# Part of one convolution job computed in float32 inside the first stage of a two-block transformer kernel

## The reference

```python
mod = silu(c) @ w_ada + b_ada                    # 2048 -> 6*2048, one row
h = rmsnorm(x, norm_mix) * (1 + sc_a) + sh_a     # 256 x 2048
p = h @ w_in                                     # 2048 -> 9296 columns
c_q, c_kv, k_pe, q_g, k_g, v_g, z, b_logit, a_logit, gate_logits = split(p)
y_a = mla(c_q, c_kv, k_pe, ...) @ w_o_mla        # latent attention, 8 heads
y_b = gdn(causal_conv_silu([q_g, k_g, v_g]), ...) @ w_o_gdn   # gated delta rule
```

## Time and profile before

| | |
|---|---|
| median of three runs | 2272.47 us |
| the profiled execution | 2270.37 us, of which the span shown in the profile is 2269.0 us |
| PE, PEld busy | 2191.9 us (97%), 1841.6 us (81%) |
| DVE, ACT, POOL busy | 1512.9 us (67%), 999.8 us (44%), 28.9 us (1%) |
| mean granted clock of TensorE | 0.989 of full |
| chain that ended last | PE 81%, DVE 9%, issue 3%, DMA 3%, ACT 3% |
| HBM | 503.56 MB read, 223 GB/s over the span |

### The profile page before, as it was taken

One profiled execution on the slowest core, in us unless ns is written; L12 is line 12 of the kernel. 1 busy time (PEld: TensorE's weight loads), 2 busy tenths in 40 slices (PEclk: granted clock), 3 DMA queues, 4 the chain that ended last, 5 costly groups with the idle time before them and its releaser, 6 DMA issues.

```text
span 2269.0 us, 27387 instructions
## 1 busy us (share of the span) xinstructions
PE 2191.9 (97%) x10608; PEld 1841.6 (81%) x10608; DVE 1512.9 (67%) x1898; ACT 999.8 (44%) x1263; POOL 28.9 (1%) x28
## 2 busy tenths in 40 slices
PE   6788999999998999999999999999999999999998
PEld 4678998788886788888888888887888888888886
DVE  7989888778867667765544555566556655655556
ACT  4355444433443464443344434456444444444444
POOL 0000000000000000000000000000000000000000
PEclk9899999999999999999999999999999999999999
DMA  9978747676899858986656556556666666566663
GB/s 361 403 260 241 253 151 268 216 252 221 268 320 263 291 199 275 297 248 214 195 189 191 190 194 191 190 192 194 194 188 194 186 195 193 184 192 191 192 190 127
DMA packets 261844, 507.87 MB, mean 224 GB/s; under 512 B 35274, under 2 KB 51410, under 8 KB 256850
## 3 DMA queue, kind: packets, MB, share of 16 engines
q1 hardware_dynamic: 261714, 506.14, 68.3%
HBM read 503.56 MB, written 2.51 MB: 223 GB/s over the span
## 4 chain that ended last, share of the span: by engine, by line
PE 81%; DVE 9%; issue 3%; DMA 3%; ACT 3%; SPq 0%; POOL 0%; DVEq 0%; ACTq 0%; POOLq 0%
PE bank L1183 24%; PE bank L1185 24%; PE bank L1184 24%; DVE WL L1951 3%; DVE RAW L1938 2%; PE bank L1128 2%; PE bank L1372 1%; DMA RAW<-in_w_o_dram 1%; PE bank L1195 1%; PE bank L1197 1%; PE bank L1196 1%; DVE A L1938 1%; ACT WH L1451 1%; DVE A L2133 1%; DMA RAW<-in_w_o_gdn_dram 0%
## 5 line engine op out<-in xcount | busy, mean ns | idle before, releaser
L1951 DVE TENSOR_TENSOR WL<-RAW,WH 128x1024 fp32r<-128x1024 f32 x715 | 867.6, 1218 | 597.8 <-ACT WH L1451 591.2
L1451 ACT CAST WH<-RAW 128x1024 fp32r<-128x1024 f32 x715 | 745.6, 1046 | 902.6 <-PE bank L1185 722.9
L1183 PE MATMUL bank<-WH,HTh 128*128 128x512 f32 x1916 | 756.4, 395 | 12.9 <-DVE WL L1951 12.3
L1184 PE MATMUL bank<-WL,HTh 128*128 128x512 f32 x1916 | 748.9, 391 | 0.0
L1185 PE MATMUL bank<-WH,HTl 128*128 128x512 f32 x1916 | 748.7, 391 | 0.0
L1183 PEld LDWEIGHTS bank<-WH,HTh 128*128 128x128 f32 x1916 | 361.8, 189 | 90.1 <-DVE WL L1951 16.5
L1185 PEld LDWEIGHTS bank<-WH,HTl 128*128 128x128 f32 x1916 | 361.5, 189 | 76.5
L1184 PEld LDWEIGHTS bank<-WL,HTh 128*128 128x128 f32 x1916 | 361.8, 189 | 72.7
L1183 PE MATMUL bank<-WH,R2h 128*128 128x512 f32 x408 | 161.7, 396 | 5.9 <-DVE WL L1951 5.9
L1185 PE MATMUL bank<-WH,R2l 128*128 128x512 f32 x408 | 159.9, 392 | 0.0
L1184 PE MATMUL bank<-WL,R2h 128*128 128x512 f32 x408 | 159.8, 392 | 0.0
(11 more groups left out here) (280 smaller groups left out, 1816.0 us busy)
## 6 DMA issues: line engine op xcount, KB each, us to landing
RAW<-in_a_w_in_dram SPq DMA_DIRECT2D x192, 512.0 KB, 3.6
RAW<-in_w_gate_up_dram SPq DMA_DIRECT2D x176, 512.0 KB, 4.5
RAW<-in_w_in_dram SPq DMA_DIRECT2D x129, 512.0 KB, 5.2
RAW<-in_w_ada_dram SPq DMA_DIRECT2D x128, 512.0 KB, 5.8
RAW<-in_w_down_dram SPq DMA_DIRECT2D x88, 512.0 KB, 4.3
RAW<-in_a_w_out_dram SPq DMA_DIRECT2D x64, 512.0 KB, 3.8
A<-in_w_ada_dram SPq DMA_DIRECT2D x18, 1024.0 KB, 8.2
RAW<-in_w_o_dram SPq DMA_DIRECT2D x32, 512.0 KB, 6.4
```

Source lines behind the costliest of these rows:

```text
L1183: e.matmul(o, ah[:, s], hi[:, k, :], start=first, stop=False)
L1184: e.matmul(o, ah[:, s], lo[:, k, :], start=False, stop=False)
L1451: e.copy(hi, rv).then_inc(S["hi"], 1)
L1951: e.tensor_tensor(lo, rv, hi.bitcast(F32), ALU.subtract).then_inc(S["lo"], 1)
```

## The change: what it does

The first stage takes three quarters of `conv` 1 as well: 384 of its 512 channels, together with the 80 small columns, 464 columns in all (`CS`). They are not split: PE multiplies the float32 weights as loaded, stationary, with the unrounded `tmp1` as the moving operand, in float32, four matmuls of 256 tokens for each K block, into banks 4 and 5. The `sm` job and its splits go. The remaining 128 channels of `conv` 1 stay a split job after the first stage, of two units of eight K blocks instead of eight units of two.

The host lays out the weights of the first stage by K block, so that each partition's part of a unit is one piece: `w_cs` (464 columns), `w_cq` (512), `w_cd` (c_kv and `conv` 0 side by side, 1024 columns, now one unit of 1 MB, split in two steps), `w_ct` (the last 128 channels). `w_cs` has two buffers of its own, and its loads wait for PE's use of the buffer (`load_cs`).

The order of the first stage: a group's `h` is made behind the next group's first modulation block on DVE and not ahead of it, `cs` (the float32 matmuls) is PE's first step of a group and needs `tmp1` alone, and in the last group all weights are split ahead of the last modulation block. At the start, DVE sums the squares of the first 128 rows behind the first quarter of `CB`, ACT those of the others ahead of its fourth tanh, the power follows, and all scaling is ACT's, in four pieces of 1024 columns; transposes begin after two of them. Latent transposes use banks 6 and 7; the small columns' transposes go into bank 1 and move to the background steps. Nine half-size reductions move in `BESIDE`: three from `conv` 1, four from `conv` 2, one from each of `uqn` 0 and 1; two more go beside each of `conv` 3, `conv` 4 and gate job 2, one beside each z job and one beside gate job `gb` 3.

```diff
+CS = 3 * P + 80
...
-    front = [Job("sm", 0, ba, 16, 80, "ht", side="ch", lazy=True),
-             Job("cq", 0, plain(win, O_CQ), 16, 512, "ht", lazy=True),
-             Job("ckv", 1, plain(win, O_CKV), 16, 512, "ht", lazy=True),
-             conv(0, O_Q)]
+    front = [Job("cq", 0, laid("w_cq"), 16, 512, "ht", lazy=True),
+             Job("ckv", 1, laid("w_cd"), 16, 512, "ht", lazy=True),
+             Job("conv", 0, laid("w_cd"), 16, 512, "ht", side="ch", lazy=True)]
...
-    a1 = [conv(1, O_Q + 512), conv(2, O_K)]
+    a1 = [Job("conv", 1, laid("w_ct"), 16, P, "ht", side="ch", step=8, lazy=True), conv(2, O_K)]
...
-BESIDE |= {("conv", 1): (3, 5, 7), ("conv", 3): (3, 7), ("conv", 4): (3, 7), ("conv", 5): (3, 7), ("ga", 2): (), ("gb", 3): (1, 3, 5),
-           ("wo", 0): (0, 1, 2, 4, 5, 6), ("wo", 1): (0, 1, 3, 5), ("gate", 0): ()}
+BESIDE |= {("conv", 1): (), ("conv", 2): (3, 7), ("uqn", 0): (1,), ("uqn", 1): (1,),
+           ("conv", 3): (1, 3, 5, 7), ("conv", 4): (1, 3, 5, 7), ("conv", 5): (3, 7), ("ga", 2): (3, 7), ("gb", 3): (1, 3, 5, 6),
+           "z": (1, 2, 3, 4, 6, 7), ("wo", 0): (0, 1, 2, 4, 5, 6), ("wo", 1): (0, 1, 3, 5), ("gate", 0): ()}
...
+        m = self.ms()
+        for n in range(4):
+            if n == 3:
+                self.put("x_sq", 1)
+                self.put("x_rs", m)
+            self.put("c", n)
+            if n == 0:
+                self.put("x_sq", 0)
+        self.put("x_sc", m)
+        self.put("xt")
+        cq, ckv, conv = jobs
+        for gi, (k0, n) in enumerate(GROUPS):
+            self.front_ada()
             if gi:
+                self.put("h", gi - 1)
+                self.put("cs", gi - 1)
                 self.front_half(cq, 0)
+                self.front_split(ckv)
+                self.front_split(conv)
+                self.front_half(ckv, 1)
+                self.front_half(conv, 3)
...
+            if gi + 1 == NG:
+                self.front_split(cq)
+                self.front_split(ckv)
+                self.front_split(conv)
+            while self.ga_n < 2 * (k0 + n):
+                self.front_ada()
             self.put("cam", gi)
+            if gi + 1 < NG:
+                self.front_split(cq)
+        self.put("h", NG - 1)
         self.put("load_cst2")
+        self.put("cs", NG - 1)
+        self.fill(1)
+        self.put("smt")
         self.front_half(cq, 0)
         lat = [self.done(cq, 0), self.done(ckv, 1)]
-        self.fill(1)
-        next(lat[0])
-        self.fill(1)
         next(lat[0])
         self.front_half(ckv, 1)
         self.fill(1)
-        next(lat[0], None)
         next(lat[1])
+        next(lat[0])
         self.front_half(conv, 3)
         self.fill(1)
-        self.pending[1] = lat[1]
-        self.bg.append(lat[1])
+        next(lat[1])
+        self.bg += lat
...
+        elif kind == "cs":
+            gi, = args
+            k0, n = GROUPS[gi]
+            W.wait_ge(f"cs_in{gi % 2}", 16 * (gi // 2) + 16)
+            W.wait_ge("xmod", k0 + n)
+            for k in range(n):
+                w = L.CS[gi % 2][:, CS * k:CS * k + CS]
+                h = L.tmp1[gi % 2][:, k * T:k * T + T]
+                first, last = k0 + k == 0, k0 + k == 15
+                e.matmul(bank[4][:, T:2 * T], w[:, 2 * P:3 * P], h, start=first, stop=last, skip_group_check=True)
+                e.matmul(bank[4][0:80, 0:T], w[:, 3 * P:CS], h, start=False, stop=last, skip_group_check=True)
+                e.matmul(bank[5][:, 0:T], w[:, 0:P], h, start=first, stop=last, skip_group_check=True)
+                i = e.matmul(bank[5][:, T:2 * T], w[:, P:2 * P], h, start=False, stop=last, skip_group_check=True)
+            i.then_inc(S["cs"], 1)
...
         elif kind == "sm_t":
             W.wait_ge("smt", 1)
-            for bb in range(2):
-                i = e.transpose(bank[4][:, 80 * bb:80 * bb + 80], L.SMT[0:80, bb * P:bb * P + P], ident[0:80, 0:80])
+            W.wait_ge("lat_c", 2)
+            for bb in range(2):
+                i = e.transpose(bank[1][:, 80 * bb:80 * bb + 80], L.SMT[0:80, bb * P:bb * P + P], ident[0:80, 0:80])
...
+        elif kind == "load_cs":
+            gi, = args
+            k0, n = GROUPS[gi]
+            W.wait_ge("cs", gi - 1)
+            e.dma_start(L.CS[gi % 2][:, 0:CS * n], a["w_cs"][:, k0:k0 + n, :]).then_inc(S[f"cs_in{gi % 2}"], 16)
...
+def first_weights(w):
+
+    def blocks(*cols):
+        v = np.concatenate([w[:, c0:c0 + n] for c0, n in cols], 1)
+        return v.reshape(16, P, -1).transpose(1, 0, 2)
+    return {"w_cs": blocks((O_Q + 512, 3 * P), (O_KPE, 64), (O_BA, 16)), "w_cq": blocks((O_CQ, 512)),
+            "w_cd": blocks((O_CKV, 512), (O_Q, 512)), "w_ct": blocks((O_Q + 512 + 3 * P, P))}
```

More of the change, by code:

```diff
@@ L363, in plan_units @@
         u = self.units
-        sm, cq, ckv, conv = jobs[:4]
+        cq, ckv = jobs[:2]
         last = ()
-        for k0, n in GROUPS:
+        for gi, (k0, n) in enumerate(GROUPS):
             g = [("g", 16 + k0 + k) for k in range(n)] + [("g", k0 + k) for k in range(n)]
@@ L415, in issue_loads @@
                 free = self.marks.get(("raw_free", s), ())
+            if u[0] == "w" and u[1].name == "cq":
+                self.put("load_cs", group_of(u[2]))
             self.put("load", i, free)
@@ L456, in front @@
         self.issue_loads()
-        sm, cq, ckv, conv = jobs
-        for gi, (_, n) in enumerate(GROUPS):
+        m = self.ms()
[9 more added lines that the diff above has]
+        cq, ckv, conv = jobs
+        for gi, (k0, n) in enumerate(GROUPS):
+            self.front_ada()
@@ L506, in front_split @@
         _, uj, t0, nkt = self.units[i]
-        assert uj is j
-        hid = len(self.halves)
+        assert uj is j or (uj.name, j.name) == ("ckv", "conv")
+        hid, c0, width = len(self.halves), 512 * (uj is not j), 1024 if uj.name == "ckv" else j.n
         place = self.free_place(j)
@@ L512, in front_split @@
         self.user[place] = hid
-        self.halves.append((j, t0, nkt, i, 0, nkt))
+        self.halves.append((j, t0, nkt, i, c0, width))
         self.put("split", hid)
+        if c0 + j.n < width:
+            return
         self.marks[("raw_free", self.raw_slot(i))] = (("lo", hid + 1),)
@@ L765, in latent_t, with small_rest @@
             yield
-    def gates(self):
+    def small_rest(self):
         yield
+        self.put("sm_t")
+        yield
+        for bb in range(2):
+            self.put("rope_k", bb)
+            yield
+        for name in ("sm_b", "sm_c", "sm_d", "sm_e"):
+            self.put(name)
+            yield
         self.put("gates")
@@ L1435, in act_program @@
         kind, args = step[0], step[1:]
-        if kind == "begin":
-            for n in range(4):
-                W.wait_ge("c_t", n + 1)
-                e.activation(L.TH[:, 512 * n:512 * n + 512], bank[n], ACT.Tanh, scale=0.5).then_inc(S["c_th"], 1)
+        if kind == "c":
+            n, = args
+            W.wait_ge("c_t", n + 1)
+            e.activation(L.TH[:, 512 * n:512 * n + 512], bank[n], ACT.Tanh, scale=0.5).then_inc(S["c_th"], 1)
         elif kind == "split":
             hid, = args
-            j, _, nk, i, k0, nkt = sch.halves[hid]
-            rv = L.raw(sch.raw_slot(i), nkt, j.n)[:, k0:k0 + nk, :]
+            j, _, nk, i, c0, width = sch.halves[hid]
+            rv = L.raw(sch.raw_slot(i), nk, width)[:, :, c0:c0 + j.n]
             hi, _ = L.halves(sch.place[hid], nk, j.n)
@@ L1479, in act_program @@
                              scale=L.cAm[:, kt:kt + 1], bias=L.cBm[:, kt:kt + 1]).then_inc(S["xmod"], 1)
-        elif kind == "sm_t":
-            W.wait_ge("half", sch.jobs["front"][0].end)
+        elif kind == "smt":
+            W.wait_ge("cs", NG)
             W.wait_ge("ht_lo", NG)
@@ L1492, in act_program @@
             c, = args
-            W.wait_ge("half", sch.jobs["front"][1 + c].end)
+            W.wait_ge("half", sch.jobs["front"][c].end)
             for bb in range(2):
@@ L2563, in sp_program @@
                 _, j, t0, nkt = u
-                for dst, src in j.loads(t0, nkt, L.raw(slot, nkt, j.n)):
+                for dst, src in j.loads(t0, nkt, L.raw(slot, nkt, 1024 if j.name == "ckv" else j.n)):
                     e.dma_start(dst, src).then_inc(S[f"raw{slot % NR1}"], 16)
```

175 lines of the change are left out of this document (68 added, 107 removed).

## The result

The changed kernel takes 2277.6 us (median of 8 runs, 2274.8 to 2281.5), the kernel before 2272.5 in the same session (8 runs): ratio 1.0023, 95% interval 1.0014 to 1.0032. It is slower by 5.1 us, where 15.5 us faster was forecast. About 5 of the 10 us between the two profiles are therefore no effect of the change.

What follows compares the result with a forecast made beforehand. Bound: DVE and DMA in the first stage, DVE and PE balanced up to `uqp`, then PE. Terms -0.6 - 16.4 + 1.5 = -15.5 us on 2270.4 give 2254.9, as a median 2257.0 us; range 2247 to 2267.

Steps and rivals of the forecast that it cites:

- part one: First stage, up to the end of the last modulation reduction: ends at 132.1 us, against 132.7 before.
- part two: From the last modulation reduction to the first `uqp` unit: lasts 69.5 us and not 85.9, a gain of 16.4.
- rival 1: First stage: PE's clock makes it slower; at 0.65, 26 us more, 2283 us in all; chance 7%.
- Rival 3: First stage: the rate stays at 401 GB/s, the stage ends 4.8 us later, 2262 us in all; chance 12%.
- The queue should stay full: 2.6 us won: Start of the first stage: seven slots and earlier first reduction keep loads flowing, winning 2.6 us.
- the hole: First stage, 18 to 24 us: DMA at 229 GB/s, put down to little-filled slots and a late first release.
- to DMA alone: First stage: its bound turns from DVE and DMA together to DMA alone, 13.2 us of DVE against 14.9 a group.
- costed at zero: First stage: SP's new wait in `load_cs` costs zero, up to 1 us a group if PE falls back.
- the bound stays where it is: DVE's work plus its waits: Part two: DVE's work of 55.3 us plus waits of 14.2, between bounds of 8 and 20.
- rival 2: Part two turns into a chain of latencies, DVE waits 22 us and more; gain 8, 2264 us; chance 12%.
- Behind part two: After the first `uqp` unit: the nine moved reductions cost 1.5 us, between bounds of 0 and 10.8.
- PE's own work is the bound: From 218.6 us on: PE busy for 376.39 of 381.40 us, nothing in the change touches it.

Runs made afterwards that it cites:

- c2_after: The changed kernel itself, unchanged, profiled a second time; its last reduction began 0.8 us earlier, at 134.2 us, and its late stretch took 244.5 us.
- e7_plain: The changed kernel without the laid-out weight copies, reading the same columns from `w_in` in smaller row pieces; 2284.6 us, ratio 1.0051.
- e11_kp_vec: e1_kp_early with the three loads of small vectors moved from the start to behind the first stage; 2266.4 us, ratio 0.9982.
- e1_kp_early: The changed kernel with the transposes of the small key columns (`kp`) put three slots earlier; 2270.6 us, ratio 0.9995.
- e2_lat_stagger: The changed kernel with the second latent's transposes two slots later; 2276.3 us, ratio 1.0019.
- e10_kp_lat: e1_kp_early with each latent's transposes two steps later and the second latent's two steps behind the first's; 2269.4 us, ratio 0.9997.
- e6_beside: The changed kernel with the extra modulation reductions back beside the weights of the kernel before; 2279.7 us, ratio 1.0029.
- e4_no_f32_conv: The changed kernel without the float32 three-quarter job of `conv` 1, extra modulation rows back where the kernel before had them; 2278.8 us, ratio 1.0025.
- e14_kp_vec_beside: e11_kp_vec with the extra modulation reductions back beside the weights of the kernel before; 2273.2 us, ratio 1.0003.

## Why the prediction was wrong

The sum on the profiled execution was 2254.9; it took 2280.3, 25.4 us more. Of these, 5.2 came in part one, 13.0 in part two and 7.2 behind it (from the first `uqp` matmul to the end 2060.4 us, where before had 2051.8 and 1.5 were allowed).

*Part one, 132.1 forecast, 137.3 measured.* The rate was right: 418 taken, 417 measured, and the clock rose from 0.84 to 0.92 as rival 1's "against" had it. PE's float32 work cost nothing until the last group; there the low clock of this execution cost 0.8 us (by c2_after). Rival 3, at 401, is refuted, and e7_plain shows what it would have been. The rule behind it (the Trainium skill, "DMA: Bandwidth & Descriptors", section Specifications: pieces of 512 B or more reach line rate) does not agree with the packet times of e7_plain, where 2048 bytes still fall short (364 GB/s against 415). Two steps failed. "The queue should stay full: 2.6 us won" read the hole as a lack of free slots; it moved from 18 to 24 us to 22 to 26 and stayed, because the small vectors cause it (e11_kp_vec: 1.9 us at the stage's end, 2.8 by the two profiles with the full clock there). And the stage does not turn "to DMA alone": at its end the last group's splits stand ahead of the last reduction on DVE, where the forecast had booked them only as a gain for what follows. The wait of `load_cs` on SP, costed at zero, did stop the queue, for 8 us here and 6 at the full clock, but e1_kp_early has 410 and 402 GB/s in spite of it, and its last reduction waits only 0.2 us for data. The zero was near right, for a wrong reason: the forecast had no wait at all.

*Part two, 69.5 forecast, 82.5 measured.* DVE's work came to 59.7 us, not 55.3. Most of the difference is no added work: with PE held up, DVE stands further ahead when the first `uqp` matmul starts. It has done 17 of the 128 x 1024 subtractions where 21 were done before, four fewer and not six, 5 half-size reductions for 13, eight fewer and not nine, and one convolution's scaling more. In e1_kp_early, without the long wait, it has done 54.2 us of work at that point, so the count was right. The step that failed is "the bound stays where it is: DVE's work plus its waits", with waits of 14.2 between bounds of 8 and 20. They were 22.8, and still 19.4 in e1_kp_early. This is rival 2's condition, at 12%, and its argument against (no single wait exceeds 3.5 us) spoke of an order of steps that the change took apart. By the runs, 9 us of the 13 were one wait of PE for one bank, for a copy behind other work on DVE, with the slow matmuls after it: without it part two lasts 73.6 us (e1_kp_early). The other 4 are waits of DVE and PE for each other and for ACT, which 14.2 put too low; no run removed them. The forecast did look at banks 6 and 7, for the latents' transposes, and not at who else uses them. Its other suspicion, the two latents' transposes in one step, was right as an observation (a wait of 4.1 us) and wrong as a cause, since spacing them moves the wait elsewhere (e2_lat_stagger, e10_kp_lat).

*Behind part two, 1.5 forecast.* The moved reductions cost 3 us between 324 and 528 us (e6_beside, e4_no_f32_conv and e14_kp_vec_beside agree), twice what was taken and well inside the bounds. The late stretch added 6 us in the pair of profiles, of which 2.8 are within the variation of the kernel before alone (237.2 and 240.0). A lead is not simply kept there, either: e1_kp_early is 7.6 to 7.9 us ahead of the kernel before at the last `nat_sq` step (316.0 us for 323.6 and 323.9) and level with it at the first `gate` eviction (830.6 for 829.8 and 831.4); 3 us of that are the moved reductions. The forecast read "PE's own work is the bound" out of a sum of waits of 15 us, of which it never asked what they would be for a PE that comes earlier.

The range was too narrow for this. The only rival above 2271 us was the clock, which rose in the first stage; the collision of two users of one bank, whose distance in steps the change shortens, was not among them.

## What to carry to other kernels

When a change takes units of work out of a hand-written order, list every pair of steps that share a bank or buffer and whose distance it shortens, and ask for each what stands ahead of the release on its engine: removed work is also removed cover. A wait that comes back at another step when it is moved is the lag of a chain; one that disappears for good was a collision, and only an experiment on the step tells them apart. When an experiment takes two things out at once, here a job and the place of nine reductions, its gain belongs to neither alone. Loads of a few bytes per partition belong where no large load is queued behind them.

## What the runs showed of the hardware

Three loads that copy the same 8, 8 and 128 values into each of 128 partitions, in pieces of at most 512 bytes, hold back the large loads queued behind them: 84 GB/s from 22 to 24 us, where the same kernel without them has 426, and 1.9 to 2.8 us at the stage's end. A long wait of TensorE is paid twice: behind 9.0 us of standing still the granted clock was 0.50 for 4 us and matmuls of 256 columns took 0.21 us from start to start instead of 0.12. And one kernel's late transfers are not equally fast in each execution: e11_kp_vec's two profiles have 239.9 and 243.5 us in the late stretch, the kernel before's 237.2 and 240.0. A difference of 3 us there, in single profiles, says nothing about a change.
